# Three of four transposes of the first gate stage moved from TensorE to VectorE and memory, in a two-layer decoder trunk on one core

## The reference

```python
for i in range(2):
    h = rms_norm(x, norm_mix[i])
    x = x + (gmlp_mixer(h, ...) if i == 0 else s5_mixer(h, ...))
    x = x + swiglu(rms_norm(x, norm_ffn[i]), ffn_w1[i], ffn_w3[i], ffn_w2[i])
    gate = sigmoid(rms_norm(x, norm_ple[i]) @ ple_w_gate[i])
    x = x + gate * (p[i] @ ple_w_proj[i])
return rms_norm(x, norm_final)
```

## Time and profile before

| | |
|---|---|
| median of 3 runs | 2237.54 us (2236.33 to 2238.45) |
| the profiled execution, its own time | 2237.34 us |
| its span in the trace | 2235.3 us |
| mean granted TensorE clock | 0.999 of full |
| TensorE busy | 2220.3 us, 99% of the span |
| VectorE, ScalarE, GpSimd busy | 1440.1, 1023.8, 494.0 us |
| moved, by HBM | 527.89 MB, mean 236 GB/s |

### The profile page before, as it was taken

The page is one execution under the profiler, slowest core; times in us unless marked ns, Lnnn a source line. Parts: engine busy times, 40 slices in busy tenths (PEclk is TensorE's granted clock), DMA queues, the critical chain, the costliest instruction groups (busy, mean ns, idle before and its releaser), DMA issues.

```text
span 2235.3 us, 28341 instructions
## 1 busy us (share of the span) xinstructions
PE 2220.3 (99%) x11250; PEld 1833.7 (82%) x11250; DVE 1440.1 (64%) x1590; ACT 1023.8 (46%) x1233; POOL 494.0 (22%) x470
## 2 busy tenths in 40 slices
PE   9999999999999999999999999999999999999998
PEld 7888888888888888888887788888888888888886
DVE  7878766767676666666668775555555445555665
ACT  5544444544434444444544454544443344444444
POOL 1256154456665544301003100000000000000001
PEclk9999999999999999999999999999999999999999
DMA  8677898888878898987779877677776667777763
GB/s 303 186 219 216 262 273 243 259 247 237 266 243 230 240 273 249 267 248 267 232 261 348 306 228 214 193 225 217 212 216 209 192 196 224 219 209 233 229 210 145
DMA packets 348517, 527.89 MB, mean 236 GB/s; under 512 B 105969, under 2 KB 125313, under 8 KB 347745
## 3 DMA queue, kind: packets, MB, share of 16 engines
q1 hardware_dynamic: 337296, 488.50, 72.5%
q0 software_dynamic: 8320, 30.75, 3.7%
q10 hardware_dynamic: 2768, 6.83, 0.9%
HBM read 474.10 MB, written 51.90 MB: 235 GB/s over the span
## 4 chain that ended last, share of the span: by engine, by line
PE 97%; DMA 1%; DVE 1%; ACT 0%; issue 0%; ACTq 0%; SPq 0%; DVEq 0%
PE PS L1590 62%; PE PS L1596 31%; DMA RAW<-in_s_w_out 1%; PE PS L1621 0%; PE PS L1863 0%; PE PS L1864 0%; PE PS L1862 0%; PE PS L1695 0%; PE PS L1684 0%; PE PS L1809 0%; DMA UP<-ud 0%; DMA RAW<-in_s_w_in 0%; PE PS L1784 0%; PE PS L1801 0%; DMA ud<-UT 0%
## 5 line engine op out<-in xcount | busy, mean ns | idle before, releaser
L1590 PE MATMUL PS<-WHI,OP 128*128 128x512 f32 x6208 | 1538.5, 390 | 0.4 <-DVE OP L1111 0.4
L1075 DVE TENSOR_TENSOR WLO<-RAW,WHI 128x1024 fp32r<-128x1024 f32 x783 | 1021.3, 1317 | 702.2 <-ACT WHI L796 697.5
L1590 PEld LDWEIGHTS PS<-WHI,OP 128*128 128x128 f32 x6208 | 1161.9, 188 | 244.1 <-issue 3.2
L796 ACT ACTIVATE WHI<-RAW 128x1024 fp32r<-128x1024 f32 x783 | 828.1, 1062 | 989.5 <-PE PS L1596 655.2
L1596 PE MATMUL PS<-WLO,OP 128*128 128x512 f32 x3104 | 829.7, 389 | 0.0
L1596 PEld LDWEIGHTS PS<-WLO,OP 128*128 128x128 f32 x3104 | 582.6, 188 | 121.0
L780 POOL TENSOR_TENSOR ON<-X,GF 128x1024 f32<-128x1024 f32 x3 | 9.9, 3298 | 944.4 <-DVE X L1424 944.4
L682 POOL TENSOR_TENSOR TA<-BRAW,FAC 128x64 f32<-128x64 f32 x16 | 9.0, 565 | 287.5 <-DMA BRAW<-in_s_b_im 287.4
L844 ACT ACTIVATE S<-PS,RC 128x512 f32<-128x512 f32 x66 | 41.7, 684 | 40.0 <-PE PS L1596 39.9
L1087 DVE TENSOR_TENSOR OP<-HT,OP 128x512 fp32r<-128x512 f32 x50 | 36.2, 765 | 12.0 <-ACT OP L811 11.9
L811 ACT ACTIVATE OP<-HT 128x512 fp32r<-128x512 f32 x50 | 28.8, 624 | 25.8 <-DMA HT<-zd 25.8
(11 more groups left out here) (214 smaller groups left out, 944.1 us busy)
## 6 DMA issues: line engine op xcount, KB each, us to landing
RAW<-in_ffn_w SPq DMA_DIRECT2D x528, 512.0 KB, 4.4
RAW<-in_gm_w_in SPq DMA_DIRECT2D x64, 512.0 KB, 3.9
RAW<-in_s_w_out SPq DMA_DIRECT2D x64, 512.0 KB, 4.5
RAW<-in_ple_w_gate SPq DMA_DIRECT2D x56, 512.0 KB, 4.3
zd<-ZT SPq DMA_DIRECT2D x37, 512.0 KB, 3.5
HT<-zd SPq DMA_DIRECT2D x148, 128.0 KB, 5.0
RAW<-in_gm_w_out SPq DMA_DIRECT2D x32, 512.0 KB, 5.5
RAW<-in_s_w_in SPq DMA_DIRECT2D x32, 512.0 KB, 5.5
```

What stands on the lines that cost most here:

```text
L796: A_.activation(hi_of(t), raw_of(t), ACT.Copy).then_inc(hi_ready, 1)
L1075: V_.tensor_tensor(lo_of(t), raw_of(t), hi_of(t).bitcast(F32), ALU.subtract).then_inc(lo_ready, 1)
L1590: T_.matmul(dst[:, th, :], x_part, hi_of(t)[:, f], start=first and kk == 0 and part == 0, stop=False)
```

## The change

The first three quads of `gate0` get bank `None`: `x` goes by VectorE's block transposes and memory, as in the other stages, and is turned by TensorE no more. The fourth quad stays with TensorE. Since the reordering of tokens now happens where `OP` is written from `HT`, the instructions are split by halves of the tokens and have their own views: they read `HT` in one run and write `OP` with a step of 32 elements (128 bytes). For each of the three quads ScalarE has eight instructions of 128x128 instead of four of 128x256, and VectorE too; VectorE's also read the high part with that step.

```diff
 def quads(stage, cols, block, row, after):
     for i, n in enumerate(cols):
-        last = i == len(cols) - 1 and stage[:2] != "up" or stage == "gate0"
+        last = i == len(cols) - 1 and stage[:2] != "up"
         at = end(stage, n) + (after if last else 6 if row is None else 7)
         QUADS.append((stage, n, i, block + 4 * i, row, at, 4 if last else None))
...
+        def steps_of(x_, h):
+            return x_.rearrange("p (j h i k) -> p h i k j", j=T, h=2, i=4)[:, h]
+
+        def tokens_of(x_):
+            return x_.rearrange("p i (k j) -> p i k j", j=T)
...
-                            if bank is None:
+                            if bank is None and stage == "gate0":
+                                for th in range(2):
+                                    last = A_.activation(steps_of(OP[:, block_ + m, 0:TOK], th), tokens_of(HT[:, :, m, th, :]),
+                                                         ACT.Identity, scale=VEC[:, row, k:k + 1])
+                            elif bank is None:
...
-                            if bank is None:
+                            if bank is None and stage == "gate0":
+                                for th in range(2):
+                                    last = V_.scalar_tensor_tensor(
+                                        steps_of(OP[:, b, TOK:2 * TOK], th), tokens_of(HT[:, :, m, th, :]), VEC[:, row, k:k + 1],
+                                        steps_of(OP[:, b, 0:TOK].bitcast(F32), th), ALU.mult, ALU.subtract)
+                            elif bank is None:
```

## The result

The changed kernel takes 2244.67 us (median of 9 runs, 2241.48 to 2246.55) against 2237.52 us before (9 runs, 2236.33 to 2238.45). The ratio is 1.0031 with a 95% interval of 1.0023 to 1.0040: slower, by 7.1 us, where 2.3 us less was forecast and the range ended at 2238.2. Of the rivals it is the first, a late root, at its far end.

The account below looks back on a forecast made before the run. TensorE, busy 99% of the span, was taken as the bound; 2.76 us of transposes removed less 0.4 us of root delay gave 2.4 us gained, a median of 2235.2 us, range 2233.2 to 2238.2.

Parts of the forecast that it names:

- the first, a late root: Rival, chance 0.13: behind column 3 `HT` comes late, delaying the root one for one; 2236 to 2239.1, or 2242.1 upward.
- The work removed: TensorE in `gate0`: three groups of eight transposes go, 0.92 us each, 2.76 us gained in all.
- I take nothing, covered by the seven buffers: SP's queue in `gate0`: load of end+8 goes about 1 us late per column, covered by six tiles of lead; cost nothing.
- 1 to 3 us: Sign to look for: SP's wait at the write (L520) grows by this much in sum.
- +6.3: `gate0`: the transposed `ZT` should be ready for SP's write 6.3 us behind the end of its column.
- the hand-over of quad 2: VectorE and ScalarE at column 3's end: high parts begin at -5.9 us, so `Z` and the root come 0.4 us late.
- the price of a late root: Seam behind column 3: each microsecond of root delay adds one to TensorE's 0.7 us wait for `UP`, with no cover.
- The stepped instructions: Quad parts: VectorE's eight taken at 0.56 us each, 3.9 us in all; ScalarE's eight at 3.0 us.
- The second: Rival, chance 0.06: 3.1 MB and SP's waits push a weight tile past its turn in columns 0 and 1; 2238 to 2241.
- The third: Rival, chance 0.08: the seam is paced by transfers, so the gain becomes waiting there; 2237.5, no change.
- The fourth: Rival, chance 0.05: TensorE's two seam waits, 0.7 and 1.5 us, vanish too; 2232.6, faster by over 0.2%.

Follow-up runs that it names:

- experiment 1: The change with the write of the three `gate0` quads two loads later in SP's queue, behind the load of end+9: 2234.50 us.
- experiment 2: The change with the quads' write and reads cut to 32 bytes a row, reads memory to memory, parts made from `Z`: 2234.00 us.
- experiment 8: The change with the write of the three `gate0` quads issued by ScalarE on its own queue: 2235.44 us.
- experiment 9: The change with the four reads of each `gate0` quad issued on ScalarE's queue, the write left on SP: 2250.55 us.
- experiment 10: The kernel before, with the statistics of the last `gate0` column taken four times on VectorE: 2244.59 us.
- experiment 13: The change with SP's wait for the root three loads later, behind the load of tile W0+9: 2237.93 us.
- experiment 6: The change with only quads 0 and 1 of `gate0` moved, quads 2 and 3 turned by TensorE: 2239.00 us.
- experiment 3: The change with the three quads' parts written by the plain forms, no 128-byte step, four high parts for eight: 2241.16 us.
- experiment 7: The kernel before, with SP waiting behind load end+7 of columns 0 to 2 for two unused VectorE block transposes: 2236.94 us.

## Why the prediction was wrong

**The work removed was right.** A turn is worth 0.92 us, and experiment 1 gains 2.8 us for three. That the two agree to a tenth is in part chance, for other waits of TensorE moved too in that experiment: `UP` (0.7 us) and `CV` (1.5) are gone, and one of 1.4 us for `YP` is new.

**First failed step: "I take nothing, covered by the seven buffers".** The seven buffers do cover TensorE: no load came past its turn there. But the held loads stand ahead of other things. SP's wait was 23.0 us where "1 to 3 us" was given. By the prediction's own +6.3 it should have been about 9, since SP reaches the write at +3.3 (1041.9 for column 0); "1 to 3" counts only what goes beyond the turn of the next load at +5.4. Counted so, the loads went 2.3, 5.9 and 8.4 us late. `ZT` was taken to be ready at +6.3 in every column. It was ready at +7.7 in the first, where a table load of 1.28 us stands ahead of the sigmoid, and later in each next one, since the parts of a quad stand ahead of the next column's `Z`. Then the loop closes: late `Z`, late write, longer hold, bigger burst, slow landing of loads and reads, late parts. Experiments 1, 2, 8 and 9 bear it out: without the hold or without the bytes the loss is gone, and another queue for the reads doesn't help.

**Second: the hand-over of quad 2.** "The high parts can begin when tile W0+1 is split, which waits for TensorE to end tile W0-4 (-8.2)" had the wrong releaser. That split waited for its load, which was held and then took 9.9 us to land, and began at +0.05: 8.2 us late. The term behind it, 1.2 us of waiting for `HT`, measured 1.27. Both had to be in time, though, for with the load alone in time the reads would have let the parts begin no sooner than +2.4, when they landed. The trace of before has a row of this kind, in `out0`, which the prediction did not use: a write for which SP had stood 6.0 us (L520 before the change), three loads in one burst behind it (L514), and the reads (L525) with their time to landing:

```profile
249.54 0.34 SPq L520 DMA_DIRECT2D zd<-ZT  x1
249.93 1.89 SPq L514 DMA_DIRECT2D RAW<-in_gm_w_out  x3
252.57 2.20 SPq L525 DMA_DIRECT2D HT<-zd  x4
...
DMA to landing us min/median/max: 7.0/7.5/8.2
```

There ScalarE waited 5.7 us for the first of the held loads; TensorE had no wait.

**Third: the price of a late root.** "Each microsecond by which the root comes later is one more on that 0.7 us wait" named the right start and the wrong path. The `UP` wait went away altogether. What is late is the turn of quad 3, by the late `X`, and then tile W0+6, by way of the loads that SP holds for the root and VectorE's order (low parts of quad 3 behind the split of W0+7), with no slack; experiments 10 and 13 show the second. And the price is 7.3 us for 3.9, not one for one: the held load also lands more slowly, and the tile behind the pause runs at 1.2 GHz.

**Not in the sum at all: the clock.** Two pauses, of 2.4 and 2.9 us, cost 3.4 us on top of themselves. The Trainium skill says in "TensorE: Matmul & The Clock Gate", Part 1, that an array that has been idle runs at 1.2 GHz instead of 2.4. The trace agrees in the level, with 0.50 granted from 1139.5 on; there the fall came a microsecond after work had begun again. Behind the 0.7 us wait for `UP` before the change the granted clock stayed at 1.00 (1163.2 to 1165.2).

**The stepped instructions** came out cheaper than taken: 0.459 us each (median) and 3.02 to 3.07 us for eight on VectorE, the price estimated for one stepped stream (0.453, 3.0), where I took two (3.9). ScalarE's eight took 2.58 us of the 3.0 taken. The Trainium skill says in "Vector Engine (DVE) Microarchitecture Reference", 5.2, that penalties for reading and for writing only partly add. Here the second stepped stream cost next to nothing, 0.006 us over that estimate for one.

**The rivals.** The first was the one, and had 0.13, with 0.03 for this size. It put the cause at a slower landing, which is so, but for a reason that could be worked out from SP's queue; and its price, one for one, was too low. The second is false as to TensorE, which waited for no load, and right in that loads came past their turn: on ScalarE. The third is false. The fourth is false for the change; in experiment 1, where both of its waits did vanish, 2.8 us were gained and not 4.9.

**The better version** is the change with the write behind the load of end+9: 2234.50 us, faster than both, and with SP's wait for the root behind W0+9 as well 2234.09 us. The two can't be told apart by these runs. Left open: what spreads the runs of experiments 6 and 13 over 6 to 9 us, and how much each link of the loop adds, for only its ends were cut. Nor did any run move GpSimd's table loads, 5.77 MB in 85 us of the same stretch, out of the way of the burst.

## What to carry to other kernels

When a queue gets a wait, price not only what the last engine in the line will feel but everything that the queue issues until it has caught up: who stands behind each late transfer, and what must land among that burst. When a handed-over piece of work stands ahead of what starts the next hand-over, work out at least three rounds: a delay that is harmless once can grow. A place without a wait can be a place without slack, as tile W0+6 was. For each hand-over compare the end of the writing with the start of the reading, and ask what it costs to be 3 us late there, the lower clock included.

## What the runs showed of the hardware

- TensorE's clock fell to its lower level at pauses of 2.4 to 5.8 us. The eight matmuls of the first part of a tile then took 3.50 us after the change and 3.67 us in experiment 10, in place of 1.98, and about 1.7 us were lost each time. With a pause of 4.3 us in experiment 3 it was more: the tile behind it took 5.29 us (1133.12 to 1138.41), 2.6 us over a plain one. The granted clock could fall in the pause (0.73 from 1133 to 1135 in experiment 10) or after it (after the change, 1.00 until 1139.5).
- Reads of 128 KB issued right behind a burst of three loads took 7.3 us (median) on SP's queue and 8.5 us on ScalarE's. With the same bytes issued 2.7 to 6.4 us after the load ahead of them, as in experiment 1, they took 4.3 us.
- The 512 KB loads of `in_ple_w_gate` took 9.0 us (median) after the change, 4.7 before, and 5.0 in experiment 7, which holds loads for a shorter time and adds no bytes.
- The same 3.9 us of work on an engine busy 64% of the time was worth 7.3 us in experiment 10 and nothing in experiment 7, by where it stood.
